# A two-block transformer kernel on one core: where the last four pieces of the modulation weights stand in the weight stream

## The reference, cut to what matters

```python
mod = c_act @ w_ada[l] + b_ada[l]
shift1, scale1, gate1, shift2, scale2, gate2 = jnp.split(mod, 6, axis=-1)
hdn = modulate(rmsnorm(x, norm1_g[l]), shift1, scale1)
proj = hdn @ w_in[l]
q_lat, c_kv, k_pe, sb_qkv, mb_qkv, gates = jnp.split(proj, SPLIT_POINTS, axis=-1)
q = to_heads(rmsnorm(q_lat, q_norm_g[l]) @ w_uq[l], N_HEADS_MLA)
kv = to_heads(rmsnorm(c_kv, kv_norm_g[l]) @ w_ukv[l], N_HEADS_MLA)
...
o_mla = from_heads(causal_softmax_attention(q_mla, k_mla, v_mla, mla_scale))
...
g_a, g_b, g_c = jnp.split(jax.nn.sigmoid(gates), N_BRANCH, axis=-1)
merged = (g_a * (o_mla @ w_o_mla[l]) + g_b * (o_sb @ w_o_sb[l]) + g_c * (o_mb @ w_o_moba[l]))
x = x + gate1[:, None, :] * (merged @ w_out[l])
hdn = modulate(rmsnorm(x, norm2_g[l]), shift2, scale2)
```

## Time and profile before

| what | value |
|---|---|
| median of three runs | 1758.13 us |
| own time of the profiled execution | 1756.55 us |
| its span (first to last instruction) | 1754.8 us |
| TensorE busy | 1693.9 us, 97% |
| VectorE busy | 1156.1 us, 66% |
| ScalarE busy | 837.8 us, 48% |
| GpSimd busy | 141.3 us, 8% |
| weights and inputs read from HBM | 321.02 MB, 184 GB/s over the span |
| mean granted clock of TensorE | 0.989 of full |

### The profile page before, as it was taken

How to read it: one execution, slowest core, us unless ns; L and a number is a source line. 1 busy time by engine, 2 the same in 40 slices (tenths; PEclk the granted TensorE clock), 3 DMA queues, 4 the chain that set the end, 5 groups by cost and what they waited for, 6 DMA issues and landing times. The chain is left out here.

```text
span 1754.8 us, 24642 instructions
## 1 busy us (share of the span) xinstructions
PE 1693.9 (97%) x9251; PEld 1378.4 (79%) x9251; DVE 1156.1 (66%) x2001; ACT 837.8 (48%) x1477; POOL 141.3 (8%) x296
## 2 busy tenths in 40 slices
PE   6999999999999999999999999999999999999998
PEld 3897675689878886774899878766998787669986
DVE  6675664865776975547735685645788766557885
ACT  3344463355443442661555354464554544645552
POOL 1210101000000000210000010141000100410000
PEclk8999999999999999999999999899999999999999
DMA  9886434557855984337466647505665566046652
GB/s 342 295 281 222 157 97 154 185 194 252 297 164 189 347 271 140 120 97 231 150 207 192 193 135 228 168 1 153 198 187 183 159 216 180 1 131 212 187 182 83
DMA packets 185911, 323.69 MB, mean 184 GB/s; under 512 B 13540, under 2 KB 101184, under 8 KB 185792
## 3 DMA queue, kind: packets, MB, share of 16 engines
q1 hardware_dynamic: 183200, 320.54, 56.3%
q10 hardware_dynamic: 2592, 1.57, 0.3%
HBM read 321.02 MB, written 1.05 MB: 184 GB/s over the span
## 5 line engine op out<-in xcount | busy, mean ns | idle before, releaser
L1787 DVE TENSOR_TENSOR ring_r<-ring,high 128x1024 fp32r<-128x1024 f32 (+3 forms) x382 | 451.5, 1196 | 283.9 <-ACT high L1355 276.2
L1355 ACT ACTIVATE high<-ring 128x1024 fp32r<-128x1024 f32 (+3 forms) x382 | 393.3, 1037 | 490.2 <-PE bank L731 354.2
L731 PE MATMUL bank<-ring_r,featT_r 128*128 128x512 f32 (+3 forms) x864 | 329.9, 382 | 0.0
L731 PE MATMUL bank<-featT_r,high 128*128 128x256 f32 x960 | 272.7, 284 | 0.0
L731 PE MATMUL bank<-featT_r,ring_r 128*128 128x256 f32 x960 | 271.7, 283 | 0.0
L731 PE MATMUL bank<-oT_r,high 128*128 128x256 f32 x960 | 271.7, 283 | 0.0
L731 PE MATMUL bank<-high,featT_r 128*128 128x512 f32 (+3 forms) x680 | 264.7, 389 | 5.8 <-DVE ring_r L1787 3.4
L731 PE MATMUL bank<-high,oT_r 128*128 128x512 f32 (+3 forms) x680 | 257.7, 379 | 0.0
L731 PE MATMUL bank<-high,gates_r 128*128 128x512 f32 x736 | 230.1, 390 | 3.4 <-DVE ring_r L1787 2.6
L731 PEld LDWEIGHTS bank<-featT_r,high 128*128 128x128 f32 x960 | 184.2, 192 | 1.0 <-DVE ring_r L1787 0.7
L731 PEld LDWEIGHTS bank<-oT_r,high 128*128 128x128 f32 x960 | 184.3, 192 | 0.3 <-issue 0.2
(11 more groups left out here) (261 smaller groups left out, 2213.7 us busy)
## 6 DMA issues: line engine op xcount, KB each, us to landing
ring<-in_w_ff SPq DMA_DIRECT2D x128, 512.0 KB, 4.7
ring<-in_w_ada SPq DMA_DIRECT2D x96, 512.0 KB, 5.8
ring<-in_w_up SPq DMA_DIRECT2D x176, 256.0 KB, 3.4
ring<-in_w_in SPq DMA_DIRECT2D x64, 464.0 KB, 5.1
ring<-in_w_in SPq DMA_DIRECT2D x48, 512.0 KB, 5.3
ring<-in_w_in SPq DMA_DIRECT2D x48, 474.0 KB, 4.6
ring<-in_w_down SPq DMA_DIRECT2D x44, 512.0 KB, 3.4
ring<-in_w_out SPq DMA_DIRECT2D x24, 512.0 KB, 5.1
```

The costliest lines, as they stand in the source:

```text
L731: ins = pe.matmul(o, a, b, start=start, stop=stop, skip_group_check=True)
L1355: act.activation(it["high"], it["raw"], ACT.Copy).then_inc(high_ready, 1)
L1787: dve.tensor_tensor(it["low"], it["raw"], it["high"].bitcast(F32), ALU.subtract).then_inc(low_ready, 1)
```

## The change

The four ada pieces leave their two places behind the halves of `w_uq` and stand together behind the gate unit, in front of the two ukv pieces. On VectorE the two ada steps ahead of `split_unit` go away, and the two steps behind the copy of uq half 0 become four. Layer 1 has no ada pieces there and is the same.

```diff
--- before.py
+++ after.py
@@ -426,9 +426,9 @@
                       spare=spare_1 if u == 0 else None)
             for u in range(2):
                 plain(*[cols_piece(w_uq[l], k0, k0 + 2, (UQ_W * u, UQ_W * u + UQ_W)) for k0 in range(0, QR // P, 2)])
-                for _ in range(0 if l else 2):
-                    ada_piece()
             gate_unit = split(w_in[l], (ATT + 2 * 512, ATT + 3 * 512), later=True)
+            for _ in range(0 if l else 4):
+                ada_piece()
             for u in range(2):
                 plain(cols_piece(w_ukv[l], 0, KVR // P, (512 * u, 512 * u + 512)))
             for it in gate_unit:
@@ -2155,8 +2155,6 @@
                 rope(qk[:, :, :, 0:8], qk[:, :, :, 8:16], 16, 8, (0, T, 2 * NH))
                 modulation_out(l, IN_OUT[l][10])
                 features_out(pcol[:, l, 16:24])
-                for _ in range(0 if l else 2):
-                    ada_step()
                 split_unit()
                 for t in range(T):
                     dve.tensor_copy(k_mla[:, t, :, NOPE:QK],
@@ -2164,7 +2162,7 @@
                 for u in range(2):
                     b = tile(for_dve)
                     read(for_dve, dve.tensor_copy(qmla[:, 1, u * UQ_W:(u + 1) * UQ_W], b[:, 0:UQ_W]))
-                    for _ in range(2 if u == 0 and l == 0 else 0):
+                    for _ in range(4 if u == 0 and l == 0 else 0):
                         ada_step()
                 for hf in range(2):
                     for t in range(T):
```

## The result

The changed kernel takes 1769.69 us (median of 4 runs, 1769.13 to 1772.13) against 1757.49 us (4 runs, 1756.10 to 1760.35) before: 12.2 us more, a ratio of 1.0064 with a 95% interval of 1.0052 to 1.0076. It is slower. The profiled execution took 1772.13 us by its own clock, with a span of 1770.4 us.

A forecast was written before the change was run, and what follows sets the result against it. The prediction took TensorE, busy 97% of the span, as the bound. Its terms 4.7 + 5.1 + 4.2 made 14.0 us later, 1772.1 us from the median 1758.13, with a range of 1764 to 1776 to hold 8 in 10.

The forecast's parts named there:

- both waits and both slow spells: Main case: TensorE waits for ukv and in the MLA softmax, half clock after each; 14.0 us later, chance 0.50.
- What gets earlier: Gate unit splits move into VectorE's 8 us pause; TensorE wins only 0.43 us, the wait for uq half 1's copy.
- First term, the ukv loads: Before ukv: both loads issued later, at 177.93 and 184.35, so TensorE ends ukv later; +4.7 us (4.1 to 5.4).
- Third term, the first spell: In the ukv matmuls: TensorE's clock falls to half after the ukv wait; +1.6 us.
- Second term, the next gate unit: MLA softmax: next gate unit's loads wait for the gate unit's uses, delaying TensorE's transposes; +5.1 us (4.0 with 4.8 us landing).
- Third term, the second spell: After the MLA softmax wait: TensorE's clock falls to half while TensorE is the bound; +2.6 us.
- the third term: TensorE's clock at half after each of the two new waits; +4.2 us together (0 to 6.2).
- That the clock stays: Rival: both TensorE waits come, but the clock stays or falls once; 9.8 us, 1767.9 (up to 1770.5), chance 0.27.
- one wait alone is left: Rival: only the ukv wait or only the softmax wait costs TensorE time; 1762.8 to 1765.8 us, chance 0.13.
- the copy of uq half 1 mattered: Rival: VectorE's copy comes in time, ukv is there at 178.54, TensorE wins 1.4 us; 1756.7, chance 0.10 including no effect.

The follow-up runs named there:

- wait_ukv: Kernel before, only SP changed: layer 0's two ukv loads issued only once the second and third pieces of uq half 1 are used; 1762.46 us, ratio 1.0022.
- warm_short: Changed kernel plus 4 and 6 extra fp32 matmuls keeping TensorE busy in its two long waits; 1766.62 us, ratio 1.0049.
- split_late: Changed kernel, but in layer 0 all four splits of the next gate unit stand in front of step 3 of the MLA softmax; 1766.00 us, ratio 1.0042.
- wait_next: Kernel before, only SP changed: the next gate unit's four loads issued only once the gate unit's four pieces are used; 1765.53 us, ratio 1.0036.
- wait_both: Kernel before, SP holding back both layer 0's ukv loads and the next gate unit's loads until the suspected pieces are used; 1768.31 us, ratio 1.0057.
- after_again: The changed kernel itself, unaltered, measured again; 1769.87 us, ratio 1.0070.
- stream_only: Changed kernel's stream with VectorE's old order: two ada steps ahead of the splits, two behind the copy of uq half 0; 1771.84 us, ratio 1.0078.
- mended: Changed kernel with ukv pieces ahead of ada pieces, four next-gate splits before softmax step 3, fourth ada step behind uq half 1's copy; 1762.09 us, ratio 1.0020.
- ukv_ahead: Changed kernel, but the two ukv pieces stand ahead of the four ada pieces in the stream; 1769.03 us, ratio 1.0063.

## Why the prediction was right

The forecast, 1772.1 us for the case with both waits and both slow spells, was 2.4 us above the median and its range held it. Measured against the median of its own group the rise is 12.2 us where 14.0 were forecast. The steps one by one:

*What gets earlier.* Right. The splits moved from 173.72 to 163.14, the copy of uq half 1 starts at 181.45 ("at about 182"), and nothing of that reached TensorE but the 0.43 us.

*First term, the ukv loads.* The mechanism is shown by wait_ukv, which makes it without the change. The issue moments came as worked out: uq starts 0.57 us earlier in this execution, and 177.93 became 177.35. The landing was 4.9 us, not 5.3. The second ukv load went out 2.08 us after the first ukv matmul began and not 1.13, because that matmul ran at half clock: in warm_short, at full clock, the same distance is 1.15 us. It landed 3.6 us later, alone.

*Third term, the first spell.* First term and spell were put at 4.7 + 1.6 = 6.3 us at the end of ukv and measured 5.1. This is where most of the error lies: the sixteen passes took 9.50 us, while 5.1 us at half clock had been worked out to 10.4. The half clock was sized well (4.8 us of it). What was too large is the price of eight passes at full clock, 3.94 us, which does not follow from the earlier trace rows: 5.39 and 1.98 us for sixteen give at most 3.7 for eight, and warm_short shows 3.70 and 3.67. Over sixteen passes that is some 0.8 us. What warm_short shows of the spell alone is 1.1 us.

*Second term, the next gate unit.* 5.1 forecast, 5.2 measured (10.3 less 5.1). Shown from two sides: split_late takes it out, wait_next and wait_both put it in. The landings of 3.7 and 6.0 us repeat those of the earlier trace rows (3.9 and 5.9). That the size fits so well is partly luck of the profiled execution: the same second load landed after 5.6 us in after_again, 5.4 in wait_both, 4.8 in stream_only and 4.7 in wait_next, and the growth between the end of ukv and step 3 was 4.8, 4.6, 3.9 and 3.9 us there. The lower bound of 4.0 us with a landing of 4.8 was needed.

*Third term, the second spell.* 2.6 us forecast. By the table it is 2.0 us over before (12.3 less 10.3), and 2.7 us against a kernel that kept its clock. It varies too: in stream_only and wait_next, whose wait was 4.6 us, the granted clock was at half for 3.4 us and the part from step 3 to behind MLA grew by 1.1 and 1.0 us; in the changed kernel, after_again and wait_both it was at half for 6.8 us, the end of the wait included, and that part grew by 2.0, 2.3 and 2.5.

*What the third term rested on.* That both spells came is shown, but the rows behind the forecast were weaker than it says. In the windows of the earlier trace rows the clock is at half from about 34.38, and the wait of 2.66 us begins at 34.47, so that fall was not made by that wait. And for the matmuls at the start the profile's column of the granted clock reads 1.00; that they ran at half is read from their durations alone. In the kernel before the clock falls twice more in the part behind the start, at 1130.1 and 1485.0, each time within a row of 32 records of 15 columns (begun at 1127.1 and 1481.9), with TensorE busy and its last wait one of 0.5 us. So no row of before showed a wait that lowers the clock; the changed kernel and the runs behind it do.

*The rivals.* That the clock stays is refuted by the windows and by warm_short; that one wait alone is left, by both timelines; that the copy of uq half 1 mattered, by stream_only, where it ends at 187.4 instead of 182.0 and the loss is the same.

*The two pages.* The rule on idle gaps in the Trainium skill, TensorE: Matmul & The Clock Gate, section "Why this matters for your kernels" (longer gaps between bursts of matmuls put the clock back to half), held in both waits, 4.41 and 5.87 us. The formula for a transfer in the Trainium skill, DMA: Bandwidth & Descriptors, section "Anatomy of one DMA" (an estimate of 3.2 us for 512 KB, for GpSimd's path and not for SP's queue), was under all landings of 512 KB read here: the shortest took 3.5 us (after_again). The prediction says that the sum would be about 1 us smaller by it; with 3.2 us for every landing its own steps give about 4.5 us for the first two terms and not 9.8.

What stays open: whether a stream order exists that uses VectorE's pause and keeps both loads early. The kernel before leaves 1.4 us at this place, 0.08%, which these measurements would not tell from noise. It also stays open why the same second w_in load landed up to 1.3 us sooner or later from run to run.

## What to carry to other kernels

In a ring of slots filled in order, the earliest moment at which a piece can be loaded is set by the piece one ring length ahead of it. Moving pieces in the list changes that for every piece up to a ring length behind, also for those that were not moved: write down for each position which use lets it go, before and after, and when its reader wants it. Never put a piece that holds its slot for long (here the gate unit, split early and used late) exactly one ring length ahead of one that is wanted soon after. And a pause of an engine at 66% is no prize when another is at 97%.

## What the runs showed of the hardware beyond what was expected

The clock also fell behind a wait shorter than those of the changed kernel. In wait_next TensorE waited 2.16 us for the first ukv load, until 181.48, and the windows around it show 0.77 and 0.80 granted. That is 1.8 and 1.6 us at half: it fell at about 182.2, when matmuls already ran again, and came back at about 185.6. In mended a wait of 1.59 us left it at 1.00:

```profile
180.00:184.00 4.00, 2.52 (x4) 1.16 (x5) 3.92 (x6) 1.81 (x3) 0.00 (x0) 0.77 0.15 57
184.00:188.00 4.00, 4.00 (x9) 1.65 (x8) 3.56 (x7) 0.00 (x0) 0.00 (x0) 0.80 0.00 0
```

```profile
184.00:188.00 4.00, 2.25 (x5) 0.68 (x4) 3.54 (x7) 0.00 (x0) 0.00 (x0) 1.00 0.04 14
```

Filling the two waits with matmuls whose results nobody reads won 3.25 us. It is a patch, but it shows that a wait of TensorE can cost more than its length, here some 3 us more on about 10 us of waiting.

A load of 512 KB issued 1.3 us behind another took 4.5 us (after_again, the first ukv load) to 6.1 us (ukv_ahead, w_in) to land, where one with nothing just ahead of it took 3.5 to 4.0, so of two loads let go in quick succession the second is the one to look at.
